# Three edits to a two-layer encoder kernel: who splits the first expert tile, where half a projection stands, and the order of w_in and w_ada loads

## The reference

```python
mod = silu(c) @ w_ada[layer] + b_ada[layer]           # six vectors sh1, sc1, g1, sh2, sc2, g2
hmix = rms_norm(x, norm_mix) * (1 + sc1) + sh1
qa, ka, va, qr, kr, vr, gr, us = split(hmix @ w_in)   # 2944 columns = 23 tiles of 128
att = chunk_attention(qa, ka, va, rel_bias)           # 6 heads of 64
ret = retention(qr, kr, vr, gr)                       # 6 heads of 64, rotary, decay
ssm = s5_ssm(us, ...)                                 # ends in z = y @ w_glu; z[:w] * sigmoid(z[w:])
x = x + g1 * (concat(_rms(att), ret, _rms(ssm)) * merge_gain) @ w_out
hffn = rms_norm(x, norm_ffn) * (1 + sc2) + sh2
x = x + g2 * peer(hffn, w_q, subkeys, u_tab, v_tab)
```

## Time and profile before

| | us |
|---|---|
| median of three timed runs | 2075.33 |
| lowest and highest | 2073.5, 2076.24 |
| the profiled execution | 2072.86 |
| its span | 2071.0 |
| PE busy | 2012.6 |
| DVE busy | 1603.9 |
| ACT busy | 1031.2 |

### The profile page before, as it was taken

How to read it: one execution, slowest core, us unless ns; L and a number is a source line. 1 busy time by engine, 2 the same in 40 slices (tenths; PEclk the granted TensorE clock), 3 DMA queues, 4 the chain that set the end, 5 groups by cost and what they waited for, 6 DMA issues and landing times.

```text
span 2071.0 us, 35035 instructions
## 1 busy us (share of the span) xinstructions
PE 2012.6 (97%) x11676; PEld 1748.0 (84%) x11676; DVE 1603.9 (77%) x3452; ACT 1031.2 (50%) x1677; POOL 238.3 (12%) x335
## 2 busy tenths in 40 slices
PE   5999999999999999999999999999999999999998
PEld 5799989888888888887788999988888888888877
DVE  8887999776888888887656679986677677678854
ACT  3225568655544444444522456785555555554433
POOL 2004446100000000000010053550000000000000
PEclk9999999999999999999999999999999999999999
DMA  9476851455778877555453478115555565554571
GB/s 372 145 271 214 248 138 64 147 183 199 280 281 304 298 284 273 193 182 211 148 174 111 153 220 239 65 55 192 190 195 182 204 221 197 187 189 176 179 241 56
DMA packets 119776, 406.94 MB, mean 196 GB/s; under 512 B 13200, under 2 KB 21264, under 8 KB 119184
## 3 DMA queue, kind: packets, MB, share of 16 engines
q1 hardware_dynamic: 113072, 381.77, 52.1%
q0 software_dynamic: 3744, 13.63, 3.4%
q10 hardware_dynamic: 2880, 10.49, 1.5%
HBM read 398.50 MB, written 7.34 MB: 196 GB/s over the span
## 4 chain that ended last, share of the span: by engine, by line
PE 73%; DVE 15%; ACT 4%; issue 4%; DMA 3%; SPq 1%; POOL 1%; DVEq 0%; ACTq 0%; POOLq 0%
PE ps L966 26%; PE ps L957 13%; PE ps L959 6%; PE ps L927 5%; PE ps L673 4%; DVE v_lo L1862 3%; PE ps L686 3%; DVE next_w_ada_ring L1907 3%; DVE u_lo L1857 2%; PE ps L935 2%; PE ps L872 1%; PE ps L873 1%; PE ps L874 1%; DVE gated L1870 1%; ACT gelu L1374 1%
## 5 line engine op out<-in xcount | busy, mean ns | idle before, releaser
L957 PE MATMUL ps<-h_hi_lo,u_hi 128*128 128x512 f32 x1696 | 617.4, 398 | 6.1 <-DVE u_lo L1857 5.8
L959 PE MATMUL ps<-h_hi_lo,u_lo 128*128 128x256 f32 x1484 | 416.8, 281 | 0.0
L957 PEld LDWEIGHTS ps<-h_hi_lo,u_hi 128*128 128x128 f32 x1696 | 319.2, 188 | 75.2 <-issue 6.5
L959 PEld LDWEIGHTS ps<-h_hi_lo,u_lo 128*128 128x128 f32 x1484 | 280.8, 189 | 8.0
L966 PE MATMUL ps<-v_hi,gated_hi 128*128 128x512 f32 x848 | 267.2, 396 | 4.9 <-DVE gated_lo L1876 3.9
L1857 DVE TENSOR_TENSOR u_lo<-weight_ring,u_hi 128x1024 fp32r<-128x1024 f32 x212 | 258.7, 1221 | 14.7 <-ACT u_hi L1363 11.6
L966 PE MATMUL ps<-v_lo,gated_hi 128*128 128x512 f32 x848 | 263.3, 392 | 0.0
L966 PE MATMUL ps<-v_hi,gated_lo 128*128 128x512 f32 x848 | 261.4, 389 | 0.0
L1862 DVE TENSOR_TENSOR v_lo<-weight_ring,v_hi 128x1024 fp32r<-128x1024 f32 x212 | 258.2, 1218 | 0.0
L1374 ACT ACTIVATE gelu<-gelu 128x256 f32<-128x256 f32 x212 | 88.7, 418 | 334.0 <-DVE gelu L1866 334.0
L1368 ACT ACTIVATE v_hi<-weight_ring 128x1024 fp32r<-128x1024 f32 x212 | 223.2, 1053 | 51.5 <-PE ps L966 51.5
(11 more groups left out here) (342 smaller groups left out, 3499.4 us busy)
## 6 DMA issues: line engine op xcount, KB each, us to landing
weight_ring<-in_u_tab_dram SPq DMA_DIRECT2D x220, 512.0 KB, 4.4
weight_ring<-in_v_tab_dram SPq DMA_DIRECT2D x212, 512.0 KB, 3.6
next_w_ada_ring<-in_w_ada_dram SPq DMA_DIRECT2D x56, 512.0 KB, 4.5
weight_ring<-in_w_in_dram SPq DMA_DIRECT2D x46, 512.0 KB, 3.6
v_tail<-in_v_tab_dram SPq DMA_DIRECT2D x44, 512.0 KB, 4.3
w_ada_ring<-in_w_ada_dram SPq DMA_DIRECT2D x40, 512.0 KB, 9.0
weight_ring<-in_w_q_dram SPq DMA_DIRECT2D x32, 512.0 KB, 5.1
u_ahead_lo<-in_u_tab_dram POOLq DMA_DIRECT2D x26, 512.0 KB, 8.5
```

Source lines behind the costliest of these rows:

```text
L957: last = mm(both, UH[:, b, k, :], HB[:, :, k, :], start=(k == 0), stop=(k == KT - 1))
L959: mm(PS[:, 4 + b, 0:T], UL[:, b, k, :], HH[:, k, :], start=False, stop=False)
```

## The change

1. The first expert tile of a layer is split by VectorE alone. Behind its last one-hots VectorE waits for the 62nd one-hot product (`w_mm`), for the load of the tile, copies the tile to `u_hi[0]` and makes `u_lo[0]`, and only then waits for `w_ev`. ScalarE no longer does that copy, and waits for the semaphore of it before its own first one (tile 1).
2. TensorE starts the scores of tiles 0 and 1 on waits for the late GELUs (which free the banks) in place of `w_ev`; it waits for `w_ev` before the first sum. The late tiles use the banks 5 - i % 2, so that the last of them is in bank 5.
3. Half `t = 0` of wide load 15 is done right behind the GLU product, before the wait for `glu_read`; the half `t = 1` stays behind the attention scores.
4. `ADA_BEHIND` for loads 15 to 18 goes from 26, 28, 30, 32 to 24, 24, 24, 28: w_in loads 16, 17 and 18 are issued ahead of w_ada rows 24 and up, rows 24 to 27 behind load 18, rows 28 to 31 behind load 19.

```diff
-        ADA_BEHIND = [16 + min(8, 2 * max(0, n - 3)) for n in range(15)] + [26, 28, 30, 32, 32, 32, 32, 32, 32, 40]
+        ADA_BEHIND = [16 + min(8, 2 * max(0, n - 3)) for n in range(15)] + [24, 24, 24, 28, 32, 32, 32, 32, 32, 40]
...
-                def project_wide(tiles):
-
+                def project_wide(tiles, halves=range(TT)):
...
-                        for t in range(TT):
+                        for t in halves:
...
-                        if a < 2:
+                        if a < 2 and TT - 1 in halves:
                             last.then_inc(wide_mm, 1)
...
                 last.then_inc(glu_mm, 1)
+                project_wide([15], (0,))
...
-                project_wide([15, 16, 17])
+                project_wide([15], (1,))
+                project_wide([16, 17])
...
-                    last = mm(PS[:, 4 + i % 2, 0:T], RAWG[i % 2][:, k, :], H32[:, k, :], start=(k == 0), stop=(k == KT - 1))
+                    last = mm(PS[:, 5 - i % 2, 0:T], RAWG[i % 2][:, k, :], H32[:, k, :], start=(k == 0), stop=(k == KT - 1))
...
                 E0 = l * NM
+                pe.wait_ge(ahead_gelu, l * AHEAD + A_TOP + A_GATE - 1)
+                scores(E0, 0, True)
+                pe.wait_ge(ahead_gelu, (l + 1) * AHEAD)
+                scores(E0 + 1, 1, l == 0)
                 pe.wait_ge(w_ev, (l + 1) * 64)
-                scores(E0, 0, True)
-                scores(E0 + 1, 1, l == 0)
                 add_experts(E0, 0, start=True)
...
-                    fn(GEG[:, i % 4, :], PS[:, 4 + i % 2, 0:T], ACT.Gelu_apprx_tanh).then_inc(ahead_gelu, 1)
+                    fn(GEG[:, i % 4, :], PS[:, 5 - i % 2, 0:T], ACT.Gelu_apprx_tanh).then_inc(ahead_gelu, 1)
...
-                u_high(E0, 0, 0)
+                act.wait_ge(u_hi, E0 + 1)
                 for e in (0, 1):
...
+                dve.wait_ge(w_mm, l * 64 + 62)
+                slot, n = expert_pos(l, 0, 0)
+                dve.wait_ge(in_ring[slot], n * 16)
+                v.tensor_copy(UH[:, 0, :, :], RING[:, slot, :].rearrange("p (k n) -> p k n", n=P)).then_inc(u_hi, 1)
+                u_low(E0, 0)
                 dve.wait_ge(w_ev, (l + 1) * 64)
-                u_low(E0, 0)
```

## The result

The changed kernel takes 2062.13 us (median of 4 runs, 2061.54 to 2065.76) against 2075.53 us before (4 runs, 2073.5 to 2076.24). The ratio is 0.9941, 95% interval [0.9923, 0.9958]: 13.4 us less. The forecast was 2063.2 us, 12.1 us less.

A forecast was written before the change was run, and what follows sets the result against it. The prediction took TensorE, busy 97% of the span, as the bound, so only its idle time pays. Gains of 4.0 + 1.6 + 2.5 + 4.05 = 12.1 us from the 2075.33 us median gave 2063.2 us, range 2059.5 to 2068.5.

The forecast's parts named there:

- A: Mixer of layer 0: with w_in loads reordered, retention scores start at 114.2 instead of 118.22; 4.0 us (2.3 to 4.2).
- B: Mixer of layer 1: the half tile fills the 1.41 us gap ahead of the attention scores; 1.6 us (1.4 to 1.8).
- C: Handover from one-hot stage to expert tiles, layer 0: first expert sum at 384.4 against 386.90; 2.5 us (1.3 to 2.8).
- D: Handover from one-hot stage to expert tiles, layer 1: 2.5 us plus 1.55 us of low clock removed; 4.05 us.
- VectorE sets the start of the retention scores: Mixer of layer 0: retention scores wait for VectorE's `att_in` at 114.15, with or without the half tile; 4.0 us gained.
- w_ada loads ahead of w_in loads 19 and 20 cost nothing: Mixer of layer 0: these w_in loads land by 112 and 116.5, wanted at about 122 and not before 125.
- rival 2: Both handovers give less, from a late u tile 2 or ScalarE starting tile 1 later: 2065.6 or 2066.5 us; 12%.
- The 6.3 us named among the signs: Both handovers: first expert sum 6.3 us behind the end of the last one-hot product, if the forecast is right.
- Rival 1: Low clock follows new gaps in layer 0's mixer or the handovers, 1.7 us each: 2064.9 or 2066.6 us; 18%.
- Rivals 3 and 4: Layer 0's mixer loses half or all its gain (2065.2 or 2067.2 us), 8%; all gains taken back later, 3%.
- Rival 5: Expert loop settles in another rhythm, slower: decides from 0.06 us more per tile over 212 tiles, 0.08 gives 2080; 3%.
- the third stretch in the prediction's range: Timed runs of the kernel before may hold a third low-clock stretch; strong end then 14.9 us gained (2060.4 us).

The follow-up runs named there:

- e9: The changed kernel run again in more rounds, nothing altered; 2063.22 us against 2076.04 before, ratio 0.9939.
- e1: The kernel before with the new order of loads alone; 2071.73 us against 2074.95 before, ratio 0.9987.
- e4: The changed kernel without the half tile; 2065.62 us against 2074.95 before, ratio 0.9951.
- e8: The changed kernel with VectorE's w_ada block of layer 0 split, two of eight rows moved behind the shifted scores; 2060.92 us, ratio to before 0.9937.
- e3: The kernel before with the handover edits alone (first tile split by VectorE, new waits, banks swapped); 2067.31 us, ratio 0.9962.
- e5: The kernel before with ten unused identity matmuls ahead of the first expert score in both layers; 2072.86 us, ratio 0.9992.
- e2: The kernel before with the half tile behind the GLU product alone; 2074.46 us against 2074.95 before, ratio 0.9994.
- e6: The changed kernel with the copy of tile 0 given back to ScalarE; 2070.71 us against 2076.05 before, ratio 0.9975.
- e7: The changed kernel with tile 1 also copied and split by VectorE; 2062.47 us against 2076.05 before, ratio 0.9944.
- e11: The changed kernel with both the split w_ada block and tile 1 split by VectorE; 2060.47 us against 2076.04 before, ratio 0.9922.

## Why the prediction was right

| term | predicted | measured |
|---|---|---|
| A, mixer of layer 0 | 4.0 | 3.9, of it 1.3 low clock |
| B, mixer of layer 1 | 1.6 | 1.7 |
| C, handover of layer 0 | 2.5 | 2.6 |
| D, handover of layer 1 | 4.05 | 4.1, of it 1.55 low clock |
| sum against the first profile | 12.1 | 12.2 from the GLU product to the end |
| median | 12.1 | 13.4, and 12.8 in e9 |

**Place A.** The step "VectorE sets the start of the retention scores" is shown three ways: the wait's releaser in the changed kernel, e1 and e4 without the half tile at the same 20.1 us, and e8, where taking two w_ada rows away moves it by 2.0. That w_ada loads ahead of w_in loads 19 and 20 cost nothing is shown by the rows of these tiles (119.42 and 128.54 in the changed kernel), which have no wait for a load. The prediction saw the low clock behind the old gap, but took the whole 118.22 - 114.2 as work that moves; 1.3 us of it were a low clock that comes and goes (e3, e5).

**Place B.** Right in mechanism and size; e4 takes it away and e2 gives it alone.

**Places C and D.** The order of events came as written. The copy costs 0.69 us, not the 1.2 taken, which changed nothing, as `u_lo` was early in either case. e6 shows that who copies is the gain. The load of u tile 2 left 1.6 us behind the first score, and ScalarE began that tile 0.1 us behind the GELU of tile 0, so rival 2 cost nothing. The 6.3 us named among the signs don't follow from the working, which gives 384.4 - 378.28 = 6.1, as measured. In D the prediction added 1.55 us for the clock as if certain. In the pair of first profiles that was so (10.2 against 8.6 us), but a gap of this kind was followed by it only three times in eight. That the sum met the first profile within 0.2 us is in this part luck: another pair of executions could have lacked 1.55 us in D and 1.3 in A.

**Rival 1** (the low clock comes back behind a new gap) had 18% and was found once in four profiles, at the price of 1.7 us named for it. **Rivals 3 and 4** are excluded by the distances and by the 12.2 us that arrive at the end. **Rival 5**, the rhythm of the expert loop, did not come with this change: from the first sum to the first of the tiles done ahead it is 594.7 us in layer 0 and 588.7 in layer 1, against 594.4 and 588.6 before. e7 and e11 show that it isn't empty: an edit ahead of the loop costs 1.0 us in a stretch where VectorE is late. Why VectorE's loop turns 0.12 us slower there was not found; it stays open.

**The median** moved by 0.6 to 1.2 us more than the trace's 12.2. The low clock fits as the reason. Of the 48 timed runs of the kernel before in the sets of e1, e5 and e9, the 18 with a mean granted clock of 0.996 took 2076.7 us on average, the 17 with 0.997 2075.4, the six with 0.998 2074.4 and the five with 0.999 2072.4. Most of them thus held more low clock than the profiled execution (0.998), as the third stretch in the prediction's range supposed. The nine runs of the changed kernel (four, and five in e9) stand higher: one at 0.997, three at 0.998, four at 0.999 and one at 1.0. At a clock of 0.999 the two kernels average 2072.45 and 2062.49 us, 10.0 apart, near the 12.2 - 1.3 - 1.55 = 9.4 that the trace gives with its two low stretches taken off. So about 9.4 us of the gain are idle time taken out, and the other 3 to 4 are low clock that comes less often. The stretches of the timed runs can't be seen one by one, and the clocks have three digits, so this stays an estimate.

## What to carry to other kernels

Before filling a gap, ask what the engine waits for next: work pulled forward into it is worth nothing when the following wait is for something that doesn't move (e2: 1.6 us gained, 1.6 us lost at the next load). In e8 the next wait was moved too, and TensorE ran through with it.

A gap in the bounding engine at a change of stage can be closed by giving the first piece of the next stage to whichever engine is done first, if memory and waits allow it to start before the stage's end; loosening the waits alone brought under 0.1 us (e6).

An idle gap of TensorE can have a second price, the low clock behind it, that appears in some executions only: here in 13 of the 25 gaps of 1.75 us and more. Count it with a chance, and compare several profiles before crediting it to an edit.

## What the runs showed of the hardware

- Behind TensorE's gaps of 1.0 to 1.72 us the granted clock fell in none of 68 cases, behind those of 1.75 to 2.01 us in 7 of 13 and behind those of 2.35 to 3.93 us in 6 of 12. It fell to about half (0.50 in the window of e1), and where the cost was measured, in places A and D and in e6 and e9, it was 1.3 to 1.7 us.
- VectorE's copy of 128x1024 float32 from SBUF to SBUF took 0.694 us, as long as one of 128x512 out of PSUM and little over half of the subtraction of the same size (1.22). The Trainium skill, in VectorE: DVE Perf Modes, § The perf-mode tier table (the rule you actually need), gives the copy of float32 in SBUF twice the rate of an operation on two tensors; the trace agrees that it is faster, with 1.22 / 0.694 = 1.76 times.
- One more copy and two more waits on VectorE ahead of its loop, with one copy fewer on ScalarE, were followed by some 0.12 us more at each turn of that loop in the stretch where VectorE is late, in both executions that have them (0.48 us in e7 and e11; 0.37 in the changed kernel, 0.39 before).
